# Twelve up units of a wide MLP made of seven block products in place of eight, with the block sums on GpSimd

## The reference, cut to what matters

```python
def sq_relu_mlp(h, w_up, w_down):
    return jnp.square(jax.nn.relu(h @ w_up)) @ w_down
...
        h2 = modulate(rmsnorm(x, norm2_g[l]), sh2, sc2)      # 512 x 1024
        x = x + g2 * sq_relu_mlp(h2, w_up[l], w_down[l])     # w_up 1024 x 4096, w_down 4096 x 1024
```

## Time and profile before

| | before |
|---|---|
| median of three runs | 1720.06 us |
| profiled execution | 1716.24 us |
| its span | 1714.40 us |
| TensorE busy | 1639.7 us (96%) |
| VectorE busy | 1206.1 us (70%) |
| ScalarE busy | 881.5 us (51%) |
| GpSimd busy | 148.1 us (9%) |
| one chunk of the MLP (chunk 2) | 88.34 us |

### The profile page before, as it was taken

How to read it: one execution, slowest core, us unless ns; L and a number is a source line. 1 busy time by engine, 2 the same in 40 slices (tenths; PEclk the granted TensorE clock), 3 DMA queues, 4 the chain that set the end, 5 groups by cost and what they waited for, 6 DMA issues and landing times.

```text
span 1714.4 us, 18936 instructions
## 1 busy us (share of the span) xinstructions
PE 1639.7 (96%) x7746; PEld 1307.3 (76%) x7746; DVE 1206.1 (70%) x1357; ACT 881.5 (51%) x994; POOL 148.1 (9%) x119
## 2 busy tenths in 40 slices
PE   5999998999999999999999999899999999999994
PEld 2768876657988888888888687778888888888883
DVE  6544875777653434343799975489899998989984
ACT  6423235443441323132633224578878788887884
POOL 0000020000000000000000100011212212122110
PEclk8999999999999999999999989889999999999997
DMA  9106721003132222322222011299999999999993
GB/s 380 72 0 235 292 97 74 0 1 140 57 123 98 99 98 76 107 88 74 75 82 89 27 50 33 97 365 417 369 372 383 372 368 362 361 380 355 384 365 114
DMA packets 54476, 322.81 MB, mean 188 GB/s; under 512 B 12529, under 2 KB 13041, under 8 KB 17778
## 3 DMA queue, kind: packets, MB, share of 16 engines
q1 hardware_dynamic: 42192, 304.76, 46.6%
q0 software_dynamic: 9216, 8.43, 2.2%
q10 hardware_dynamic: 2978, 8.37, 1.2%
HBM read 323.60 MB, written 23.07 MB: 202 GB/s over the span
## 4 chain that ended last, share of the span: by engine, by line
PE 90%; DVE 5%; ACT 2%; DMA 2%; issue 1%; POOL 0%; SPq 0%; ACTq 0%; POOLq 0%; DVEq 0%
PE ps L538 33%; PE ps L1355 21%; PE ps L1382 10%; PE ps L717 3%; PE ps L693 2%; PE ps L1244 2%; PE ps L956 2%; PE ps L1341 2%; DVE scr L2360 2%; PE ps L750 1%; DMA xT<-in_x 1%; PE ps L673 1%; PE ps L1364 1%; PE ps L820 1%; PE ps L863 1%
## 5 line engine op out<-in xcount | busy, mean ns | idle before, releaser
L2050 DVE TENSOR_TENSOR wlo<-raw,whi 128x2048 fp32r<-128x2048 f32 x268 | 606.4, 2284 | 157.5 <-ACT whi L1433 157.4
L1433 ACT ACTIVATE whi<-raw 128x2048 fp32r<-128x2048 f32 x268 | 507.9, 1910 | 235.4 <-PE ps L538 122.3
L538 PE MATMUL ps<-hH,whi 128*128 128x512 f32 x544 | 216.3, 398 | 0.3 <-ACT dmax L1865 0.3
L538 PE MATMUL ps<-hL,whi 128*128 128x512 f32 x544 | 214.8, 395 | 0.0
L538 PE MATMUL ps<-hH,wlo 128*128 128x512 f32 x544 | 214.8, 395 | 0.0
L1355 PE MATMUL ps<-whi,xH 128*128 128x512 f32 x512 | 205.8, 402 | 1.4 <-DVE xL L2159 1.4
L1355 PE MATMUL ps<-whi,xL 128*128 128x512 f32 x512 | 201.7, 394 | 0.0
L1355 PE MATMUL ps<-wlo,xH 128*128 128x512 f32 x512 | 200.2, 391 | 0.0
L538 PEld LDWEIGHTS ps<-hH,whi 128*128 128x128 f32 x544 | 102.1, 188 | 24.8 <-ACT dmax L1865 0.4
L538 PEld LDWEIGHTS ps<-hH,wlo 128*128 128x128 f32 x544 | 102.0, 188 | 24.9
L538 PEld LDWEIGHTS ps<-hL,whi 128*128 128x128 f32 x544 | 102.1, 188 | 24.6 <-issue 0.2
(11 more groups left out here) (480 smaller groups left out, 2814.2 us busy)
## 6 DMA issues: line engine op xcount, KB each, us to landing
raw<-in_experts SPq DMA_DIRECT2D x192, 1024.0 KB, 7.7
raw<-in_streamed SPq DMA_DIRECT2D x92, 1024.0 KB, 4.8
xT<-in_x SPq DMA_DIRECT2D x1, 2048.0 KB, 17.4
h_scratch<-hN ACTq DMA_DIRECT2D x4, 512.0 KB, 2.6
sum_scratch<-xN ACTq DMA_DIRECT2D x1, 2048.0 KB, 12.9
out<-Y SPq DMA_DIRECT2D x4, 512.0 KB, 2.7
ctxT<-in_ctx SPq DMA_DIRECT2D x1, 1024.0 KB, 18.7
Y<-sum_scratch SPq DMA_DIRECT2D x2, 512.0 KB, 5.7
```

The costliest lines, as they stand in the source:

```text
L538: ins = e.matmul(o, l, r, start=(i == 0), stop=(i == len(prs) - 1))
L1433: e.activation(u.hi, u.raw, ACT.Copy).then_inc(*p.inc("hi", n, on="hi"))
L2050: e.tensor_tensor(u.lo, u.raw, u.hi.bitcast(F32), ALU.subtract).then_inc(*p.inc("lo", n, on="lo"))
```

## The change: seven block products

For the up units of chunks 1 to 3 (twelve of sixteen), the product of a 1024 x 256 weight unit with the 1024 x 512 activations is cut into 2 x 2 blocks on each side (weights A, activations B) and made of seven block products in place of eight, in the form with few additions (Winograd's form of Strassen's scheme). Each block product is four k-tiles x three passes = 12 matmuls of 256 columns, so a unit is 84 of them in place of 48 of 512 columns.

- GpSimd makes four sums of the activations once (`t`, nine instructions of 128 x 1024 elements, after chunk 0's up units), and four sums of the weight blocks for each unit (`s1` to `s4`, 128 x 512 elements each). The sums lie in the half of `hH` and `hL` that is read no more; each sum has one buffer, so a unit's sum waits until VectorE has made the low part of the same sum of the unit before.
- ScalarE and VectorE split seven blocks (128 x 512) in place of one unit (128 x 2048). The three pairs of halves become a ring of 12 blocks of 1024 elements; a down unit takes four blocks of it. Steps are numbered (`STEPS`: seven for an up unit, four for a down unit), and `ready(last)` splits all up to a step, 11 ahead of the one in use.
- After the products, VectorE puts the output together from four PSUM banks in five sums (`u2s`, `w34`, `c22`, `c11`, `c1221`), with one copy by ScalarE (`p1s`). Then ScalarE takes ReLU, square into `UH` and square in place over 1024 elements at once, and VectorE subtracts for `UL`. `UH` and `UL` are single now.

```diff
+    STEPS = [(n, None, 4 * c + 3) for c, n in enumerate(U_DN[0])]
...
+            STEPS += [(n, j, STEP_AT[n] + j) for j in range(7)] if n in WINOGRAD else [(n, None, STEP_AT[n] + 3)]
@@ pe_program @@
+        def seven(ch, c, n):
+            a = ps.take(("a", ch, c), ("dve", "u2s", ch, c))
+            b = ps.take(("b", ch, c), ("dve", "c22", ch, c))
+            d = ps.take(("d", ch, c), ("dve", "c11", ch, c))
+            f = ps.take(("f", ch, c), ("dve", "c1221", ch, c))
...
+            def product(j, bank, half, right):
+                hi, lo, _ = units[n].blocks[j]
+                p.wait_ge(*done(*block_low(n, j)))
+                for k in range(4):
+                    for i, (l, r) in enumerate(tri((hi[:, k, :], lo[:, k, :]), (right[0][:, k, :], right[1][:, k, :]))):
+                        ins = e.matmul(bank.t[:, hs(half)], l, r, start=(k == 0 and i == 0), stop=(k == 3 and i == 2))
+                ins.then_inc(*p.inc("block", n, j))
@@ act_program @@
+        def seven(ch, c, n):
+            g = STEP_AT[n]
+            p.wait_ge(*done("pe", "block", n, 1))
...
+            copy(p1s, ps["a", ch, c].t[:, 0:256], p.inc("p1s", ch, c))
+            for j in range(6):
+                ready(g + j + 11)
+            p.wait_ge(*done("dve", "c1221", ch, c))
+            e.activation(quad, quad, ACT.Relu).then_inc(*p.inc("r", ch, c))
...
+            e.activation(UH[:, 2 * c:2 * c + 2, :], scr[:, :, :], ACT.Square).then_inc(*p.inc("uh2", ch, c))
+            e.activation(quad, quad, ACT.Square).then_inc(*p.inc("us", ch, c))
+            ready(g + 17)
@@ dve_program @@
+        def seven(ch, c, n):
+            g = STEP_AT[n]
+            a, b, d, f = (ps[x, ch, c].t for x in "abdf")
+            ready(g + 11)
...
+            TT(u2s, a[:, 256:512], p1s, ALU.add, "u2s", ch, c)
+            ready(g + 12)
+            if c:
+                lower_pair(ch, c - 1)
+            p.wait_ge(*done("pe", "block", n, 3))
...
+            e.tensor_tensor(w34, b[:, :].rearrange("p (i t) -> p i t", i=2), u2s.unsqueeze(1).broadcast_to([P, 2, 256]),
+                            ALU.add).then_inc(*p.inc("w34", ch, c))
+            ready(g + 13)
...
+            TT(quad[:, 768:1024], b[:, 0:256], w34[:, 1, :], ALU.add, "c22", ch, c)
+            ready(g + 14)
...
+            TT(quad[:, 0:256], d[:, 0:256], p1s, ALU.add, "c11", ch, c)
+            ready(g + 15)
+            ready(g + 16)
+            p.wait_ge(*done("pe", "block", n, 6))
+            TT(quad[:, 256:768], f[:, :], sqs[:, :], ALU.add, "c1221", ch, c)
+            ready(g + 17)
+            if c == 3:
+                lower_pair(ch, c)
@@ pool_program @@
+        for n in WINOGRAD:
...
+            for name, out_, a, b, op in (("s1", S1, a21, a22, ALU.add), ("s2", S2, S1, a11, ALU.subtract),
+                                         ("s3", S3, a11, a21, ALU.subtract), ("s4", S4, a12, S2, ALU.subtract)):
+                if last:
+                    p.wait_ge(*done(*block_low(last, BLOCKS.index(name))))
+                sub(out_, a, b, op, name, n)
+            last = n
```

More of the change, by code:

```diff
@@ L379, in build @@
     third = half_ring[2]
+    WINOGRAD = {n: ch for ch in range(1, 4) for n in order["up", ch]}
+    BEHIND = {n for ch in range(1, 4) for n in order["dn", ch]}
     for i, (name, k0, k1, n0, n1) in enumerate(table):
@@ L390, in build @@
         w = (k1 - k0) * (n1 - n0)
+        if i in WINOGRAD:
+            u = units[stream(A["streamed"][i, :, 0:w], k1 - k0, n1 - n0, False)]
+            c = order["up", WINOGRAD[i]].index(i)
+            if i == order["up", 1][0]:
+                block_user.update({(h.off - O_HL) // 1024 + j: ("pe", "use", h.last.n) for h in half_ring for j in range(4)})
+            first = (half_ring[0].off - O_HL) // 1024 + 7 * c
+            u.split, u.blocks = True, []
+            for j in range(7):
+                b = (first + j) % 12
+                hi = at("bhi", O_HL + 1024 * b, [4, 128], FR)
+                u.blocks.append((hi, at("blo", O_HL + 1024 * b + 512, [4, 128], FR), block_user[b]))
+                block_user[b] = ("pe", "block", i, j)
+            if c == 3:
+                half_ring.append(half_ring.pop(0))
+            continue
         stream(A["streamed"][i, :, 0:w], k1 - k0, n1 - n0, name != "dfts" and i not in unsplit)
+        if i in BEHIND:
+            b0 = (units[i].half_off - O_HL) // 1024
+            units[i].half_keys = sorted({block_user[b0 + j] for j in range(4)})
+            block_user.update({b0 + j: ("pe", "use", i) for j in range(4)})
     U_MOD = {j: order["mod", j] for j in range(12)}
@@ L450, in build, with block_source, block_low @@
     wkvb = at("wkvb", PH + 15232, [1024])
-    UH = [at("UH", PH + 8192 * i, [8, 512], FR) for i in range(2)]
-    UL = [at("UL", PH + 8192 * i + 4096, [8, 512], FR) for i in range(2)]
+    UH, UL = at("UH", PH, [8, 512], FR), at("UL", PH + 4096, [8, 512], FR)
+    TH = [at("TH", PH + 8192 + 2048 * i, [4, 256], FR) for i in range(4)]
+    TL = [at("TL", PH + 9216 + 2048 * i, [4, 256], FR) for i in range(4)]
+    freed = [at("freed", O_HH + 4096 * i, [DK, T])[:, 0:4, 256:512] for i in (1, 0)]
+    tsum = [freed[0], freed[1], freed[0], freed[1]]
+    S1, S2, S3, S4 = (freed[i // 2][:, :, 128 * (i % 2):128 * (i % 2) + 128] for i in range(4))
+    p1s, u2s, w34 = rst[:, 0:256], rst[:, 256:512], sqs.rearrange("p (i t) -> p i t", i=2)
+    quad = scr.rearrange("p m t -> p (m t)")
+    def block_source(n, j):
+        r = units[n].raw
+        return (r[:, 0:4, 0:128], S2, S1, S3, r[:, 4:8, 0:128], r[:, 4:8, 128:256], S4)[j]
+    def block_low(n, j):
+        return ("dve", "lo", n) if j == 6 else ("dve", "low", n, j)
     up, acc = at("up", PH, [4, 542]), at("acc", PH + 2168, [4, 512])
@@ L2513, in dve_program, with ready @@
                ALU.subtract, "wif", q)
+        step = [0]
+        def ready(last):
+            while step[0] < len(STEPS) and STEPS[step[0]][2] <= last:
+                n, j, _ = STEPS[step[0]]
+                step[0] += 1
+                if j is None:
+                    if n >= at_[0]:
+                        convert(n)
+                    continue
+                at_[0] = n + 1
+                hi, lo, _ = units[n].blocks[j]
+                p.wait_ge(*done("act", "high", n, j))
+                TT(lo, block_source(n, j), hi.bitcast(F32), ALU.subtract, *block_low(n, j)[1:])
```

135 lines of the change are left out of this document (114 added, 21 removed).

## The result

The changed kernel takes 1731.39 us (median of 5 runs, 1729.16 to 1735.63) against 1720.06 of the kernel before on the same chip: ratio 1.0075, 95% interval 1.0054 to 1.0096. The ratios here are of mean times: it is slower by 0.75%, some 13 us, and the medians lie 11.3 us apart. The forecast was 1729.0 (range 1711 to 1741). The profiled execution took 1729.16, span 1727.4 against 1714.40.

A forecast was written before the change was run, and what follows sets the result against it. TensorE, busy 96% of the span, was taken as the bound. Saving -15.5, ScalarE-VectorE ring +9.3, GpSimd's hold +15.8 and clock +1 gave +10.6 us; centred on 1718.4, that forecast 1729.0 us, range 1711 to 1741.

The forecast's parts named there:

- TensorE's saving: Twelve up units of chunks 1 to 3: 84 short matmuls take 9.89 us instead of 11.18 per unit, -15.5 us.
- The ring: ScalarE and VectorE from one c1221 to the next: 11.4 us against TensorE's 9.89; waits of 1.2 and 1.9, +9.3 us.
- GpSimd's hold and the clock: Up units: GpSimd's sums block VectorE's two-SBUF-input subtractions, +15.8 us; slower TensorE clock after the wait, +1 us.
- Seven of nine meetings: Per chunk nine GpSimd sums fall in the ScalarE-VectorE ring; seven hold VectorE 0.75 us each, 5.3 per chunk.
- the one of 0.60 us: Attention row before the change: 8-element VectorE instruction took 0.60 us beside GpSimd, 0.23 alone; taken as evidence of a hold.
- Rival (a): Up units: GpSimd does not hold VectorE, so the kernel gets faster: -6.2 us, 1712; chance 0.22.
- Rival (b): Up units: VectorE always wins and GpSimd's sums stretch: -2 us, 1716, no change that can be told; chance 0.10.
- Rival (c): Up units: GpSimd becomes the bound from about 1.45 us per sum; at 1.5 about +20, 1738 or more; chance 0.10.
- Sum: Whole kernel: -15.5 + 9.3 + 15.8 + 1 = +10.6 us, on the profiled execution 1726.8.

The follow-up runs named there:

- early_late_no_sums: Changed kernel with step g+17's copy before the c1221 wait, second down unit's split behind c1221, GpSimd's up-unit block sums left out: stretch 259.78 us, chunk 1 82.96.
- no_sums: Changed kernel with GpSimd's four block sums per up unit left out, raw weight blocks used instead: stretch 268.11 us, chunk 1 85.73.
- late: Changed kernel with only VectorE's splitting of the second down unit moved behind the fourth unit's c1221: 1733.1 us, ratio 1.0073, stretch 286.36.
- eight: Changed kernel with the sixth block product's twelve matmuls made twice in each of the 12 up units: 1729.1 us, ratio 1.0050, chunk 1 91.32.

## Why the prediction was right, step by step

- *TensorE's saving*, -15.5 us: in early_late_no_sums, where nothing else is in the way, the three chunks are 16.1 us shorter. Units of 39.42/4 = 9.86 us, 9.89 forecast. Right.
- *The ring*, +9.3: no_sums less early_late_no_sums, 268.11 - 259.78 = **+8.3**. Right in place and size. Without GpSimd's sums c1221 starts at 556.22, 567.72 and 577.42: turns of 11.50 and 9.70 us, 11.4 and 9.7 forecast. The wait before the down projection costs 0.9 us from start to start, 1.2 forecast; the other 1.9, as forecast.
- *GpSimd's hold and the clock*, +15.8 and +1: the changed kernel less no_sums, 285.44 - 268.11 = **+17.3** against 16.8. Of that, three times 5.6 is the longer wait before the first down unit (16.8, where 15.8 was forecast for the hold), and 0.5 the clock. The wait costs 6.3 us from start to start (6.5 forecast). The form of the second part was wrong: two waits per chunk were forecast, 6.5 and 1.9. The clock cost 2.2 us in the first down unit, more than I gave it, but thereby it stands in the place of the second wait; late shows that the two don't add up.
- *How much is held.* Seven of nine meetings at 0.75 us was 5.3 a chunk. The trace has it close to that: nine sums start in chunk 1's up phase (548.33 to 571.70), and six hold a block subtraction, those of 552.72, 554.78, 556.75, 558.22, 566.51 and 571.88, for 1.12, 0.77, 0.52, 0.99, 1.16 and 0.99 us, 5.6 in all. The first four make the first c1221 start 4.6 us behind its unit's last matmul in place of 1.2, the other two make the first turn 13.66 us in place of 11.50; the second keeps 9.70. The block subtractions between 540 and 800 us are 35 x 1.179 + 48 x 0.750 - 83 x 0.684 = 20.5 us longer than undisturbed, 6.8 a chunk, the `wlo` ones 0.7 more, and 5.7 reach TensorE. That mass sits in the subtractions from raw (1179) and hardly in those from sums (750), which the prediction did not tell apart. GpSimd's busy time grew by 255.6 - 148.1 = 107 us, not 83: its own instructions are held as well. Of the two rows behind this term, the one of 0.60 us was an instruction with one tensor and a column, so not of the form that is held here; no row of before had the pair itself. That it transferred is shown by the runs, not by the rows.
- *Rival (a)*, no hold: 1712 was its time, and with the hold taken out the stretch is 7.8 us shorter than before, 6.2 forecast. As a number it was right for a kernel without this term. *Rival (b)*, VectorE wins always, falls with the rows at 571.88. *Rival (c)*: GpSimd's sums take 1.3, below its limit of 1.45 when undisturbed, and 1.49 to 1.79 with the holds; still TensorE never waits inside the up units, and eight finds the same chunk.
- *Sum.* +10.6 was forecast for the profiled execution, the stretch has +9.5, the span +13.0. The other 3.5 are outside: 2.1 before the down projection of chunk 0 (503.55 against 501.44), 1.4 behind the stretch. In the nine experiments, none of which changes anything ahead of it, that projection starts between 500.80 and 504.56: it is a spread of single executions.

## What to carry to other kernels

Fewer matmuls are worth their time only while the chain through the other engines is shorter than TensorE's new time; add that chain from one sum to the next of its kind, in program order, with what each engine waits for. Here two moves in order (a copy ahead of a wait, a split behind one) took 24.7 us from the stretch, more than the saved matmuls' 16.1. GpSimd instructions that read SBUF are cheap only where VectorE has slack, or doesn't read two SBUF tensors beside them: the sums cost 5.7 us a chunk in a full ring and 0.3 in one with slack.

## What the hardware showed that I had not expected

- GpSimd's one-input read (1.57 us) holds a two-input VectorE subtraction by 0.46 us at most and lets it go before its own end, its two-input read (1.3) holds it by up to 1.17, until its end; its memsets not at all (684 ns beside them, the same as without GpSimd).
- Cutting GpSimd's sums in two made the stretch 5.4 us shorter, though it made GpSimd's own work longer.
- A slow clock after a long wait can be free, when what comes next would have waited anyway: 13.1 us at a clock of 0.87, and, in eight, 10.9 with waits of 1.6 and 0.5 behind up units 5.8 us longer, end the chunk at the same time.
